# Attention units scored two at a time, with the weights' release, the merging and the start laid out anew, in a decoder layer on one core

## The reference, cut to what matters

```python
h = rmsnorm(x, attn_norm)
proj = h @ w_in                       # 1024 x 3584: three dilated groups A, then B, then M's queries
o_a = dilated_mixture_attn(qkv_a)     # 3 groups (window, dilation) = (128,1) (512,4) (2048,16), 4 heads of 64
o_b = sink_swa_gqa(b_q, b_k, b_v)     # 8 query heads of 64 on 2 key heads, window 128, a sink per head
o_m = memory_attn(m_q, mem)           # 4 heads of 128 into 256 memory tokens
```

## Time and profile before

| | |
|---|---|
| median of 3 runs | 1781.49 us (1780.1 to 1785.8) |
| profiled execution | 1781.02 us, span 1779.2 us |
| first part (to the first gate product) | 0 to 620.58 us |
| TensorE busy over the span | 1698.0 us, 95% |
| VectorE, ScalarE, GpSimd busy | 860.9, 637.8, 869.7 us |

### The profile page before, as it was taken

One profiled execution on the slowest core, in us unless ns is written; L12 is line 12 of the kernel. 1 busy time (PEld: TensorE's weight loads), 2 busy tenths in 40 slices (PEclk: granted clock), 3 DMA queues, 4 the chain that ended last, 5 costly groups with the idle time before them and its releaser, 6 DMA issues.

```text
span 1779.2 us, 22678 instructions
## 1 busy us (share of the span) xinstructions
PE 1698.0 (95%) x8625; PEld 1380.5 (78%) x8625; DVE 860.9 (48%) x1353; ACT 637.8 (36%) x1151; POOL 869.7 (49%) x672
## 2 busy tenths in 40 slices
PE   6988999989889799999999999899999999999999
PEld 5876877867668688888888887788888888788887
DVE  5554233247974502210055346888888888621101
ACT  4445455445454423322111323334334333422110
POOL 6542555643412122222134646989999999222221
PEclk9998999999999999999999999999999999999999
DMA  6113001011210043333155630223223222544411
GB/s 210 36 57 92 7 19 56 1 36 38 60 36 1 3 120 95 98 99 98 62 184 165 235 100 36 83 83 93 73 72 95 83 71 86 173 140 142 144 46 64
DMA packets 131256, 151.09 MB, mean 85 GB/s; under 512 B 16780, under 2 KB 97356, under 8 KB 131148
## 3 DMA queue, kind: packets, MB, share of 16 engines
q1 hardware_dynamic: 131148, 149.63, 26.5%
HBM read 116.98 MB, written 32.62 MB: 84 GB/s over the span
## 4 chain that ended last, share of the span: by engine, by line
PE 62%; DVE 1%; POOL 1%; ACT 0%; issue 0%; ACTq 0%; DVEq 0%; POOLq 0%
PE ps L2306 23%; PE ps L1659 15%; PE ps L2391 13%; PE ps L1675 6%; PE ps L1691 5%; POOL f_lo L2147 0%; PE ps L1684 0%; DVE ffn_area L2264 0%; DVE attn_lo L2256 0%; DVE t_all L2174 0%; DVE ffn_area L1644 0%; DVE attn_out L2209 0%; DVE attn_out L2206 0%; POOL ffn_area L2163 0%; POOL ffn_area L2165 0%
## 5 line engine op out<-in xcount | busy, mean ns | idle before, releaser
L2147 POOL TENSOR_TENSOR f_lo<-ffn_area,f_hi 128x1024 fp32r<-128x1024 f32 x85 | 201.0, 2383 | 22.1 <-ACT f_hi L2034 22.0
L2306 PE MATMUL ps<-t_all,f_hi 128*128 128x512 f32 x528 | 164.1, 392 | 2.0 <-DVE t_all L2174 1.6
L1659 PE MATMUL ps<-act_hi,g_hi 128*128 128x512 f32 x384 | 151.9, 396 | 3.1 <-DVE g_lo L1592 3.1
L2179 POOL TENSOR_TENSOR attn_lo<-ffn_area,attn_lo 128x512 fp32r<-128x512 f32 x44 | 58.5, 1330 | 194.4 <-ACT attn_lo L2096 194.3
L1557 POOL TENSOR_TENSOR g_lo<-g_raw,g_hi 128x1024 fp32r<-128x1024 f32 x23 | 55.3, 2406 | 201.0 <-ACT g_hi L1467 201.0
L1659 PE MATMUL ps<-act_hi,g_lo 128*128 128x512 f32 x384 | 151.2, 394 | 0.0
L1659 PE MATMUL ps<-act_lo,g_hi 128*128 128x512 f32 x384 | 149.7, 390 | 0.0
L2034 ACT ACTIVATE f_hi<-ffn_area 128x1024 fp32r<-128x1024 f32 x85 | 80.2, 946 | 188.7 <-PE ps L2306 178.2
L2306 PE MATMUL ps<-act_hi,f_hi 128*128 128x512 f32 x336 | 133.6, 398 | 4.6 <-POOL f_lo L2147 4.6
L634 POOL TENSOR_SCALAR head_rstd<-head_ss 128x8 f32<-128x8 f32 (+2 forms) x42 | 8.3, 199 | 262.4 <-DVE head_ss L911 262.1
L1190 PE MATMUL ps<-w_hi,act_hi 128*128 128x512 f32 (+1 forms) x320 | 123.4, 385 | 10.3 <-POOL act_lo L437 5.3
(11 more groups left out here) (260 smaller groups left out, 4349.6 us busy)
## 6 DMA issues: line engine op xcount, KB each, us to landing
ffn_area<-in_w_up_dram SPq DMA_DIRECT2D x44, 512.0 KB, 5.2
gates<-gate SPq DMA_DIRECT2D x24, 512.0 KB, 3.1
gate<-gates SPq DMA_DIRECT2D x24, 512.0 KB, 3.8
g_raw<-in_w_gate_dram SPq DMA_DIRECT2D x23, 512.0 KB, 4.6
z<-attn_out SPq DMA_DIRECT2D x22, 512.0 KB, 2.6
ffn_area<-in_w_down_dram SPq DMA_DIRECT2D x22, 512.0 KB, 4.2
ffn_area<-z SPq DMA_DIRECT2D x44, 256.0 KB, 3.0
attn_out<-in_x_dram SPq DMA_DIRECT2D x16, 512.0 KB, 5.2
```

The costliest lines, as they stand in the source:

```text
L1659: ins = pe.matmul(ps[:, u % 4, :], w[:, n % 3, k, :], a[:, k, HALF[half]], start=(k == 0 and i == 0), stop=(k == NK - 1 and i == 2))
L2147: pool.tensor_tensor(part_place(p, part, f_lo, first_lo), part_source(p, part), part_place(p, part, f_hi, first_hi).bitcast(F32), ALU.subt ...
L2179: pool.tensor_tensor(z_lo[:, m % 2, :], z_raw[:, m % 4, :], z_hi[:, m % 2, :].bitcast(F32), ALU.subtract).then_inc(z_lo_done, 1)
L2306: ins = pe.matmul(out, w, a, start=(start and k == 0 and i == 0), stop=(stop and k == 3 and i == 2))
```

## The change

Units are joined to **pairs** (`PAIRS`): a step scores four heads, 1 step a job in A and M (k = 1), 2 in B (k = 0 and 4). `score(n)` and `weigh_values(n-2)` stand together; the probabilities of pair n-1 are turned apart, one unit at a time, at the k's of `TURNS_BEHIND`. The minima, exponentials and divisions of a pair are issued in one go, and the copies out take both units. In the last job of a stage b lags by `LAST_BEHIND` (1 in A, 3 in B); what is released after k = 7 is cast and subtracted in the next job behind that job's squares and sums. The 12 merge batches are spread over eight jobs. Slices of stage M come into three places of `w_raw` of 512 columns each. At the start four slices are loaded and cast before the second tile of x, the positions before the last two slices, `x_low(0)` goes from GpSimd to VectorE, `x_low(1)` and a scaling go ahead of the angles, and TensorE turns the identity 18 times behind the first tile of x.

```diff
-UNITS_OF = {"memk": 0, "memv": 0, "A": 2, "B": 4, "M": 2}
+PAIRS_OF = {"memk": 0, "memv": 0, "A": 1, "B": 2, "M": 1}
...
-              [whole(6), whole(7), W0, W1] * 4 +
-              [W0, W1, whole(2), whole(4)] * 2)
+              [whole(6), whole(7), W0, W1] * 4)
 def raw_place(n):
-    return RAW_PLACES[n - 8]
+    return RAW_PLACES[n - 8] if n < 48 else (n % 3, 1)
...
 def step_slices(j):
+    kind = KIND[j - LAG] if 0 <= j - LAG < NJ else None
+    if kind in ("A", "M"):
+        return [1]
+    if kind == "B" or j >= LAG and PAIRS_OF[KIND[j - LAG - 1]]:
+        return [0, 4]
+    return []
+TURNS_BEHIND = {1: (3, 5), 0: (1, 3), 4: (5, 7)}
+DIVIDE_BEHIND = {"A": 0, "B": 2, "M": 3}
+def turn_at(j):
+    return (7, 7) if j == 0 else (5, 7) if KIND[j] == "B" else (6, 7)
 B_BEHIND = {"A": 3, "B": 6}
+LAST_BEHIND = {"A": 1, "B": 3}
...
-        MERGE_AT = [(merge_from + 2 + m // 3, (1, 3, 5)[m % 3]) for m in range(12)]
+        MERGE_AT = [(merge_from + d, k) for d, k in ((2, 2), (2, 6), (3, 2), (4, 2), (5, 2), (6, 2), (7, 2),
+                                                     (8, 2), (8, 4), (8, 6), (9, 2), (9, 4))]
...
@@ ScalarE; VectorE has the same with sum_squares and w_low
                 if 0 <= j - 1 < NJ:
                     squares(j - 1)
+                for n in released(j - 1, 7):
+                    cast_slice(n)
...
@@ VectorE at the start
             for h in range(2):
                 x_gain(0, h)
+            x_low(dve, 0)
             w_low(dve, 3)
...
-            angles()
             x_low(dve, 1)
             x_scale(2)
+            angles()
             reduce_angles()
-            x_scale(3)
...
@@ TensorE
             for h in range(2):
                 turn_x(0, h)
+            for _ in range(18):
+                pe.transpose(ps[:, TQ, 0:P], ident[:], ident[:])
...
+                for u in range(2):
+                    for b in range(0 if has_prev(j) else 1, 1 if kind == "M" else 2):
+                        for e in range(2):
+                            rows = slice(64 * e, 64 * e + 64)
+                            ins = pe.matmul(scores[:, u, e, b * P:(b + 1) * P], q_ring[rows, j % RQ, 2 * v + u, :],
+                                            k_ring[rows, (j - 1 + b) % RK, kk, :], start=True, stop=True)
...
                         if k in step_slices(j):
+                            n = steps_before(j) + step_slices(j).index(k)
                             at(score, n)
-                            at(weigh_values, n - 3)
-                            at(turn_probs, n - 2)
+                            at(weigh_values, n - 2)
...
+                        if k in prob_turns(j):
+                            u, i = prob_turns(j)[k]
+                            at(turn_probs, steps_before(j) + i - 1, u)
```

More of the change, by code:

```diff
@@ L95, in raw_group, with shared @@
     first = raw_place(n)[0]
-    return first // 2 if first < 4 else 2 + first - 16 if first >= 16 else 3 if first == 8 else 5
+    if n >= 48:
+        return 7 + first
+    return first // 2 if first < 4 else 2 + first - 16
 def raw_before(n):
     def pieces(m):
-        return set(range(raw_place(m)[0], sum(raw_place(m)))) if m >= 8 else set()
-    return next((m for m in range(n - 1, -1, -1) if raw_group(m) == raw_group(n) or pieces(m) & pieces(n)), None)
+        if m < 8:
+            return set()
+        first, pieces = raw_place(m)
+        if m >= 48:
+            return {0, 1, 2, 3}
+        return set(range(first, first + pieces))
+    def shared(m):
+        return raw_group(m) == raw_group(n) or (pieces(m) & pieces(n) and not (m >= 48 and n >= 48))
+    return next((m for m in range(n - 1, -1, -1) if shared(m)), None)
 def raw_uses(n):
@@ L178, in low_on_pool, with released @@
     return n in (0, 2, 4, 6, 7)
-def released(kind, step):
-    last = "b" if kind in B_BEHIND else "a"
+def released(j, step):
+    if not 0 <= j < NJ or not is_last(j) or j == NJ - 1:
+        return []
+    last = "b" if KIND[j] in B_BEHIND else "a"
     done = []
-    for part, k, ended in parts(kind):
-        done += [k] if part == last else []
+    for part, k, ended in parts(j):
+        done += [8 * (JOBS[j][0] + 1) + k] if part == last else []
         if step in ended:
@@ L428, in x_split, with x_low_on_pool @@
         def x_split(eng, n):
-            eng.wait_ge(x_lo_even, (n + 1) // 2)
-            eng.wait_ge(x_lo_odd, n // 2)
+            even = sum(x_low_on_pool(m) for m in range(n))
+            if even:
+                eng.wait_ge(x_lo_pool, even)
+            eng.wait_ge(x_lo_dve, n - even)
+        def x_low_on_pool(n):
+            return n % 2 == 0 and n > 0
         def x_low(eng, n):
@@ L574, in _ @@
                     store_factors()
[L575 to L579, removed]
+                    load_factors(0)
+                    load_factors(1)
+                if n in (8 * 6 + 3, 8 * 6 + 5):
+                    load_factors(2 if n == 8 * 6 + 3 else 3)
                 if n == 8 + 2:
@@ L762, in exps @@
             def exps(n):
[L763 to L765 removed]
+                j, v = PAIRS[n]
+                kind = KIND[j]
                 c0 = 0 if has_prev(j) else P
[L767 to L774 removed]
@@ L790, in _ @@
             x_square(0)
-            for k in range(3):
+            for k in range(4):
                 cast_slice(k)
@@ L794, in _ @@
             x_square(1)
-            for k in range(3, 8):
+            for k in range(4, 8):
                 cast_slice(k)
@@ L799, in _ @@
             x_square(3)
-            n = 0
             for j in range(NJ + LAG + 1):
@@ L1294, in _ @@
                     pe.wait_ge(x_gained, 8)
-                for part, slice_, ended in (parts(KIND[j]) if j < NJ else [(None, None, [k]) for k in range(8)]):
+                for part, slice_, ended in (parts(j) if j < NJ else [(None, None, [k]) for k in range(8)]):
                     if j < NJ:
```

323 lines of the change are left out of this document (157 added, 166 removed).

## The result

The changed kernel takes 1758.1 us (median of 4 runs, 1756.0 to 1764.4), the kernel before 1780.8 us (4 runs, 1779.7 to 1785.8): ratio 0.987, 95% interval 0.984 to 0.990. It is faster by 23 us, where I had said 52. The profiled execution took 1756.0 us with a span of 1754.2, which is 25.0 us less than in the earlier trace rows.

What follows compares the result with a forecast made beforehand. TensorE was taken to bound the kernel inside stages, with stops and a falling clock at stage changes and VectorE bounding B to M. Terms summed to 50.8 us, rounded up to 52: 1781.0 - 52 = 1729 us, range 1712 to 1752.

Steps and rivals of the forecast that it cites:

- the pair: Steps of A and B: changes of form and way in once instead of twice, 0.47 us per pair, 40 pairs, 18.8 us.
- changes of stage: Where one stage's weights replace another's: slices freed one per k, last casts standing behind, shorten TensorE's stops; 30.8 us.
- start, to the fourth tile: 14.9 to 56.5 us: earlier first product and second tile, full clock if turns raise it; gain 3.8, bounds 1.2 and 6.0.
- inside A, first two B tiles: A stretches and two B tiles before 406 us: 21 pairs at 0.47 us each, gain 9.9 us.
- A to the memory stages: 123 to 168.3 us: four memory jobs, two pairs' attention, 2 us for waits; 36.3 of 45.3 us, gain 9.0.
- into A group 1: 168.3 to 183.6 us, no attention: products, drain and 2 us for waits make 10.9 of 15.3 us, gain 4.4.
- A group 1 to 2, 2 to B: 262.8 to 282.1, 362.3 to 380.5 us: 13.2 each, gains 6.1 and 5.0, less 2 each for subtractions beside GpSimd copies: 7.1.
- B: 406 to 476.4 us: TensorE bounds at 15.4 us per job, 0.8 for waits; 62.4 of 70.4 us, gain 8.0.
- B to M: 476.4 to 533.2 us: VectorE and GpSimd's rotation behind its norms bound; 46.5 us job by job, gain 10.3.
- the end: 596.2 to 620.6 us: the last pair's second unit waits behind the first's exponentials, last values for both; 1.7 us longer.
- rival 4: A pair's longer chain makes TensorE wait at fixed turns; decides from 1.3 us per pair, 1809 us at 2; chance 0.03.
- rival 2: A lone turn costs a drain, 0.18 us, 96 times: 17 us, cancelling work saved; 1746 us; chance 0.27 shared with another rival.

Runs made afterwards that it cites:

- the reordered version: Changed kernel with first unit's copy and queries' copy ahead of the exponentials, merge batches behind slice 4's minima, slice 4's divisions behind the keys' copy: 1731.6 us, ratio 0.972.
- The alternating kernel: Changed kernel with a pair's step ordered scores, values of the first unit, then scores, values of the second: 1771.2 us, ratio 0.994.
- the one with the copy first: Changed kernel with ScalarE's copy of the first unit's turned probabilities issued ahead of the next pair's exponentials: 1743.6 us, ratio 0.980.
- the third such step: Slice 4's divisions moved behind the keys' copy, against the kernel with queries' copy ahead and merge batches behind slice 4 (1744.4 us): 1731.6 us.
- the second: Queries' copy also moved ahead of the exponentials, against the kernel with only the first unit's copy ahead (1743.6 us): 1745.2 us, ratio 0.979.

## Why the prediction was wrong

The sign and the mechanism of the pair were right, and so were the stretches inside A and two of the terms for changes of stage; the total was off by 27 us. The terms of the sum against the changed kernel and against the reordered version (the divisions behind the keys' copy), each as the length before less the length after:

| stretch | said | changed | reordered |
|---|---|---|---|
| start, to the fourth tile | 3.8 | 1.9 | 1.6 |
| inside A, first two B tiles | 9.9 | 9.0 | 9.7 |
| A to the memory stages | 9.0 | 3.1 | 7.9 |
| into A group 1 | 4.4 | 4.4 | 4.4 |
| A group 1 to 2, 2 to B | 7.1 | 7.0 | 14.2 |
| B | 8.0 | 3.3 | 5.7 |
| B to M | 10.3 | 3.4 | 9.9 |
| inside M | 0 | -1.4 | 0.0 |
| the end | -1.7 | -5.4 | -3.0 |
| from the gate on | 0 | -0.3 | 0.5 |
| sum | 50.8 | 25.0 | 50.9 |

The lengths of before that the earlier trace rows lacks are these, and behind them four rows of the reordered version:

```profile
56.50:123.00 66.50, 65.80 (x483) 54.97 (x481) 32.17 (x83) 33.18 (x82) 33.74 (x51) 1.00 0.13 41
...
282.10:362.30 80.20, 79.79 (x531) 65.28 (x529) 25.53 (x94) 41.77 (x100) 48.51 (x62) 1.00 0.11 32
...
380.50:406.00 25.50, 25.07 (x169) 19.74 (x167) 12.45 (x53) 10.66 (x39) 11.33 (x16) 1.00 0.01 1
...
533.20:596.20 63.00, 62.27 (x361) 52.26 (x359) 32.52 (x75) 27.74 (x77) 14.96 (x18) 1.00 0.00 1
```
```profile
118.40:155.80 37.40, 34.16 (x228) 26.58 (x229) 22.06 (x48) 22.95 (x48) 13.58 (x16) 1.00 0.30 92
...
368.20:432.90 64.70, 62.09 (x516) 53.03 (x514) 51.08 (x164) 32.13 (x106) 22.65 (x32) 0.97 0.15 39
432.90:479.80 46.90, 41.63 (x351) 33.44 (x350) 40.81 (x120) 27.87 (x82) 14.54 (x19) 1.00 0.18 52
479.80:542.80 63.00, 62.15 (x363) 51.73 (x361) 36.90 (x68) 27.00 (x79) 14.89 (x18) 1.00 0.07 18
```

**The step that failed** is in rival 4: "the copy of unit 0 stands behind the next pair's exponentials on ScalarE. If TensorE waits there, everything queued behind it, projections too, waits". I named the mechanism and gave it 0.03, since I asked only if a pair's own chain comes late for its turn, which wanted "an error of 3.3 us in the chain". The copy isn't late by its own pair. It is queued behind the next pair's minima and exponentials, and for that the room is the two slices between the turns, 1.4 to 2.1 us, against 2.1 us of exponentials after a wait for the minima. I had all of these lengths. And I took the rival as one that applies to every pair or to none, where it applied to 17 places and should have been a term of the sum. Changing that order alone gave back 14 us, and 26 us together with the two places behind it in B, so this is shown, not argued. The two causes work together, though: with most of the merge left out and the order unchanged, 10 us came back as well, probably because the minima ahead of the exponentials were ready sooner. In the terms of the sum, B had 0.8 us for waits and TensorE stood idle for 4.5 (67.10 less 62.57).

The reordered version's 50.9 against my 50.8 is partly luck: it gives 7.1 us more than I said at the two changes between A's groups and B, and less at the start, in B, at the end and into the memory stages.

**The pair** saved nearly what I had said: 9.0 of 9.9 us inside the stages (9.7 in the reordered version), 2.17 us for scores and values of a pair of B, lone turns without a drain (0.35 us to the next product and 0.09 more for that one, 0.44 together, as in the kernel before), so rival 2 is out. The alternating kernel shows that changes of form are most of what is saved. There are 36 steps with both changes, not 40, and they cost 0.31 us, not 0.37.

**The changes of stage.** In the reordered version the lengths came near my forecast: 37.4 for 36.3, 10.9 for 10.9, 46.9 for 46.5, and 12.0 and 11.3 for 13.2 each, so the 2 us that I took off both for subtractions beside a copy on GpSimd weren't due. That the changed kernel gave 7.0 of the 7.1 there is luck: a wait of 2.3 us for the copy in each stood where I had those 2 us. My reason for the lengths was only partly right: undoing the release costs 6 to 8 us in all, and undoing its even part costs nothing in the changed kernel. What else shortened them (pairs, fewer and later instructions on VectorE, new places for M's slices) I haven't taken apart.

**B.** In three B tiles of the reordered version VectorE is busy for 37.38 of 46.30 us and TensorE is never idle, so VectorE's work does not bound it. The waits there were three in a row, each hidden by the one before: the probabilities' copy, the queries' copy, the keys' copy.

**The start** gave 1.9 of 3.8. The first product came at 13.8 us as I had said, its low part taking 1.23 us on VectorE, and the followers at full clock. The 13.8 is partly luck: over the profiles of all these kernels it lies between 13.5 and 15.4, and the first scaling takes 0.75 or some 2.3 us. The second tile then started 5.1 us earlier (24.3 for 29.4), as I had said. That lead had shrunk to 1.9 by the fourth tile, since the turn of the fourth tile's x alone waits 2.3 us (in the list's second row) for its scaling. Without the 18 turns nothing changes there.

**The end** cost 5.4 and not 1.7. From the last projection product to the gate, in the kernel before, the changed one and the one with the copy first:

```profile
595.80:620.60 24.80, 14.93 (x103) 12.65 (x101) 12.29 (x29) 10.12 (x26) 2.46 (x3) 1.00 0.05 1
```
```profile
565.10:595.30 30.20, 18.55 (x111) 15.62 (x109) 10.63 (x19) 10.15 (x26) 2.48 (x3) 0.89 0.03 1
```
```profile
555.10:581.30 26.20, 15.68 (x111) 13.40 (x109) 11.65 (x23) 10.01 (x26) 2.48 (x3) 1.00 0.04 1
```

With the copy first the loss is 1.4 us, close to my 1.7. The other 4 us are waits for the copy and the clock. Of three such waits in the changed kernel's tail (3.07, 1.98 and 0.78 us), the first two stand behind exponentials and are 0.78 each with the copy first; the third has none ahead of it and stays. The clock falls to 0.89, so that the same products are busy for 18.55 us instead of 15.68.

## What to carry to other kernels

When two units of work are joined, go through each engine in its own order and ask of every short instruction for which another engine waits (a copy, a division) what now stands ahead of it, and whether that one waits for something else; compare this with the smallest distance between the two points on the waiting engine, not with the typical one. When a mechanism that you name can apply in some places and not in others, put it into the sum place by place. And when a reorder removes a wait and the time stays, look for the same pattern at the next consumer before you give it up: here the third such step gave 12 to 13 us, where the second had given none.

## What the runs showed of the hardware that I had not expected

Turns of the identity raised TensorE's clock from its half level of 1.2 GHz to 2.4: the products behind them follow by 0.23 us, and by 0.43 without them. The profile's own column of granted clock reads 1.00 in both.

The same scaling of 128x1024 on VectorE took 0.75 us in one profile and 2.29 in another, where a subtraction on GpSimd had begun 0.07 us ahead of it, and the whole start moved by 1.6 us with it.

The granted clock goes with part of the spread within one kernel. The five runs of the kernel with the copy first took 1740.0 to 1748.2 us; the fastest had a mean clock of 0.992, the slowest 0.986. It is not the whole of it: two runs of the changed kernel at 0.986 took 1756.0 and 1764.4 us. The tails above show what a lower clock costs: the same 110 or so products are busy for 15.68 us at 1.00 and for 18.55 us at 0.89.
